# Spreading projection and gate units over two attention phases, and summing squares on another engine, in a hybrid decoder layer

## The reference

```python
z = rmsnorm(x, g_mix) @ w_in        # split: mq mk mv | mo | mi mf | fq fk fv | ff | ga gb
fq, fk = rmsnorm(fq, g_qn), rmsnorm(fk, g_kn)      # per head of 64
# mLSTM, per head and chunk of 128 positions
w_intra = exp(dlog - m_t[..., None]);  w_inter = exp(a - m_t)
s = einsum('bhtd,bhsd->bhts', q, k) * w_intra
num = w_inter * einsum('bhtd,bhde->bhte', q, c_st) + einsum('bhts,bhse->bhte', s, v)
den = w_inter * einsum('bhtd,bhd->bht', q, n_st) + sum(s, -1)
h = num / maximum(abs(den), exp(-m_t))
c_new = decay * c_st + einsum('bhs,bhsd,bhse->bhde', w_s, k, v)
# attention, per head and block of 128 queries
logits = einsum('bthd,bshd->bhts', qb, k) * F_SCALE + fb - f_keys      # causal
yf = einsum('bhts,bshd->bthd', softmax(logits), v)
# merge, FFN, embedding
hm = rmsnorm(y_m, g_mh) * sigmoid(mo)
x = x + (sigmoid(ga) * (hm @ w_pa) + sigmoid(gb) * (yf @ w_pb)) @ w_out
gu = rmsnorm(x, g_ffn) @ w_gu
x = x + (silu(gu[..., :D_FF]) * gu[..., D_FF:]) @ w_down
y = x + sigmoid(rmsnorm(x, g_ple) @ w_ple_gate) * (p @ w_ple_proj)
```

## Time and profile before

| | us |
| --- | --- |
| median of 3 runs (lowest, highest) | 2348.0 (2345.8, 2350.44) |
| the profiled execution, its own time | 2341.82 |
| its span in the trace | 2340.2 |
| TensorE busy in the span | 2082.0 (89%) |
| DVE, ACT, POOL busy | 886.7, 534.1, 575.8 |

### The profile page before, as it was taken

How to read it: one execution, slowest core, us unless ns; L and a number is a source line. 1 busy time by engine, 2 the same in 40 slices (tenths; PEclk the granted TensorE clock), 3 DMA queues, 4 the chain that set the end, 5 groups by cost and what they waited for, 6 DMA issues and landing times.

```text
span 2340.2 us, 33231 instructions
## 1 busy us (share of the span) xinstructions
PE 2082.0 (89%) x12507; PEld 1902.8 (81%) x12507; DVE 886.7 (38%) x1525; ACT 534.1 (23%) x845; POOL 575.8 (25%) x391
## 2 busy tenths in 40 slices
PE   2999997999968988947788999999999999998888
PEld 2877776999957777734687989999999999998688
DVE  4500001323346666642374323443344433444433
ACT  5212112221144454411532220011000110001311
POOL 0312222111122131100222242323223232320521
PEclk9999998998989898967899999999999999999999
DMA  3222215443222222146632121111111111100121
GB/s 120 68 80 108 88 43 165 131 138 114 76 55 77 63 72 63 49 157 217 206 117 64 36 72 37 44 46 42 47 36 54 36 54 36 45 27 27 48 71 37
DMA packets 203827, 179.44 MB, mean 77 GB/s; under 512 B 49114, under 2 KB 168126, under 8 KB 203746
## 3 DMA queue, kind: packets, MB, share of 16 engines
q1 hardware_dynamic: 154594, 151.28, 20.5%
q10 hardware_dynamic: 48160, 27.40, 3.9%
q0 software_dynamic: 1024, 0.13, 0.1%
HBM read 141.68 MB, written 39.26 MB: 77 GB/s over the span
## 4 chain that ended last, share of the span: by engine, by line
PE 76%; DVE 8%; issue 7%; ACT 2%; DMA 2%; POOL 2%; SPq 1%; ACTq 1%; DVEq 0%; POOLq 0%
PE pair L2164 23%; PE bank L2164 19%; PE bank L1860 9%; PE bank L1887 7%; PE pair L1860 4%; PE pair L2001 2%; PE pair L1975 1%; DVE dd L1475 1%; PE pair L1985 1%; PE pair L1974 1%; DVE ptl L1522 1%; PE pair L2054 1%; POOL tmp L949 1%; PE pair L1963 1%; DVE XR L1789 1%
## 5 line engine op out<-in xcount | busy, mean ns | idle before, releaser
L2164 PE MATMUL bank<-acth,wha 128*128 128x352 f32 x640 | 213.3, 333 | 30.0 <-DVE actl L1683 17.1
L2164 PE MATMUL bank<-actl,wha 128*128 128x352 f32 x640 | 210.5, 329 | 0.0
L2164 PE MATMUL bank<-acth,wla 128*128 128x352 f32 x640 | 210.5, 329 | 0.0
L2164 PE MATMUL pair<-hh,whb 128*128 128x352 f32 x528 | 173.5, 329 | 24.2 <-DVE XR L1789 23.7
L915 POOL CAST wha<-raw 128x1024 fp32r<-128x1024 f32 x46 | 52.1, 1132 | 523.2 <-PE pair L2164 190.5
L1887 PE MATMUL bank<-acth,fwh 128*128 128x352 f32 x480 | 172.2, 359 | 3.4 <-POOL fwl L835 3.4
L2164 PE MATMUL pair<-hl,whb 128*128 128x352 f32 x528 | 169.2, 320 | 0.0
L2164 PE MATMUL pair<-hh,wlb 128*128 128x352 f32 x528 | 169.2, 320 | 0.0
L1789 DVE TENSOR_TENSOR XR<-XR,pair 128x352 f32<-128x352 f32 x264 | 134.2, 518 | 81.4 <-PE pair L2164 81.2
L1887 PE MATMUL bank<-actl,fwh 128*128 128x352 f32 x480 | 165.0, 344 | 0.0
L1887 PE MATMUL bank<-acth,fwl 128*128 128x352 f32 x480 | 164.5, 343 | 0.0
(11 more groups left out here) (422 smaller groups left out, 5066.9 us busy)
## 6 DMA issues: line engine op xcount, KB each, us to landing
raw<-in_w_gu SPq DMA_DIRECT2D x44, 512.0 KB, 3.9
wraw<-in_w_in SPq DMA_DIRECT2D x24, 512.0 KB, 4.8
scratch_zA<-stage SPq DMA_DIRECT2D x48, 256.0 KB, 2.0
raw<-in_w_down SPq DMA_DIRECT2D x22, 512.0 KB, 3.3
scratch_zT<-fout ACTq DMA_DIRECT2D x20, 528.0 KB, 2.7
fraw<-in_w_in SPq DMA_DIRECT2D x20, 512.0 KB, 4.3
gs<-scratch_zT SPq DMA_DIRECT2D x16, 528.0 KB, 3.5
kpg<-in_cache_k SPq DMA_DIRECT2D x32, 256.0 KB, 4.8
```

The source lines that it names most:

```text
L2164: ins = nc.tensor.matmul(out, w[i](k), x[j](k), start=n == 0, stop=n == total - 1)
```

## The change

Phase 1 keeps 27 of the projection units, the three groups of the mLSTM. The 27 units of the attention's q, k, v (`f_unit`) run two ahead of the meeting before phase 2, one behind it, and the others in the mLSTM heads, where the nine gate units of each head stood. Their weights lie in a ring of five pieces; the first four are split in phase 1, the other eight by POOL alone (`split_unit_weights`, a copy and a subtraction a piece). In phase 2 SP loads q and k ahead of v, and the rows right behind.

All 60 gate units go to phase 3: four ahead of the first head and seven in each, as 14 halves. Their weights have two buffers instead of three; the stores of the gates go from ACT's queue to SP's, together with those of `yb`. The low part of the keys, `klo`, gets 128 rows.

In phase 5 POOL adds up the squares in `rv` (`sum_squares`), and three products with ones at the end replace L2207 and L2212. In phase 7 pin is loaded early; the low part on DVE and the squares on ACT run within the last FFN group; POOL splits the first embedding weights and then adds up the squares of two thirds of the columns, the last third goes through ones as before; the first two units of products run ahead of the sums. Loops of TensorE, ACT, POOL and SP in phases 1 to 3 and the last one of TensorE are written out.

The core of the diff, by phase and engine.

Phase 2, TensorE:

```diff
+            pe.wait_ge(unit_out, MG * XTILES)
+            f_unit(0)
+            f_unit(1)
             begin_phase(pe, 2)
+            f_unit(2)
...
+            for g in range(HM):
+                u0, wide = 7 * g, 7 * g + 6 < UNITS
+                if g:
+                    f_unit(u0)
+                pe.wait_ge(qk_in, 64 * g + 64)
...
-                gate_unit(g, 0, 3)
-                gate_unit(g, 1, 3)
+                if g:
+                    f_unit(u0 + 1)
+                    f_unit(u0 + 2)
...
-                for f in range(6, 9):
-                    gate_unit(g, f, 3)
```

Phase 2, POOL:

```diff
+            pool_mlstm(0)
+            split_unit_weights(4)
+            pool_mlstm(1)
+            for n in range(5, 9):
+                split_unit_weights(n)
+            pool_mlstm(2)
+            for n in range(9, 12):
+                split_unit_weights(n)
+            pool_mlstm(3)
```

Phase 3, SP:

```diff
+            for g in range(HF):
+                for u in range(PRE + 7 * g if g else 0, PRE + 7 * g + 7):
+                    if u % 3 == 2:
+                        store_gate(u // 3)
+                        if u // 3 + 3 < NGATE // 3:
+                            load_gate(u // 3 + 3)
+                    if u == PRE + 7 * g + 4 and g:
+                        store_y(g - 1)
+                if g < HF - 1:
+                    load_row(g + 1)
```

Phase 3, TensorE and DVE:

```diff
                 logits3(g, 2)
                 turn_p3(g, 0)
+                gate(h + 3)
                 logits3(g, 3)
                 turn_p3(g, 1)
+                gate(h + 4)
...
-                nc.vector.tensor_tensor(klo[:], pB[0:DH, :], khh[0:DH, :].bitcast(F32), ALU.subtract).then_inc(qk_lo, 1)
+                nc.vector.tensor_tensor(klo[:], pB[:], khh[:].bitcast(F32), ALU.subtract).then_inc(qk_lo, 1)
```

Phase 5, POOL and TensorE:

```diff
+            def sum_squares(first, wait):
+                for t in range(NT):
+                    pool.wait_ge(sq5, wait + t + 1)
+                    nc.gpsimd.tensor_tensor(rv[:, t, :], rv[:, t, :], sqt[:, t, :], ALU.add).then_inc(sq5_add, 1)
...
+                    split_piece(g * 2 + 10 + j, g + 6, j, wha[:, j], wla[:, j])
+                    sum_squares(j, g * 6 + 3 * j)
...
-                    if u == 3:
-                        sums(0)
-                sums(1)
```

Phase 7, POOL:

```diff
-                nc.gpsimd.tensor_tensor(sqt[:, n % 3, :], x, x, ALU.mult).then_inc(sq7, 1)
+            for j in range(2):
+                ple_weights(0, j)
+            for m in range(2 * (KC - 1)):
+                t, c = m // (KC - 1), m % (KC - 1) + 1
+                pool.wait_ge(sq7, t * KC + c + 1)
+                nc.gpsimd.tensor_tensor(rv[:, t, :], rv[:, t, :], sqt[:, m % 3, :], ALU.add).then_inc(sq7_add, 1)
```

More of the change, by code:

```diff
@@ L360, in program @@
         nst_t = sem("nst_t")
-        fw_in = [sem(f"fw_in{i}") for i in range(3)]
+        fw_in = [sem(f"fw_in{i}") for i in range(2)]
         f_hi = sem("f_hi")
@@ L1974, in logits3 @@
                     nc.tensor.matmul(out[:, c:c + w], q, khh[:, c:c + w], start=True, stop=False)
-                    ins = nc.tensor.matmul(out[:, c:c + w], q[0:DH, :], klo[:, c:c + w], start=False, stop=not last)
+                    ins = nc.tensor.matmul(out[:, c:c + w], q, klo[:, c:c + w], start=False, stop=not last)
                     if last:
@@ L2032, in pe_head @@
                 values3(g, 2)
+                gate(h + 11)
+                gate(h + 12)
                 turn_p3(g, 7)
-                gate(2, 1)
+                gate(h + 13)
                 values3(g, 3)
             pe.wait_ge(consts, 3)
-            with pe.Fori(0, HF - 1) as g:
+            for h in range(2 * PRE):
+                gate(h)
+            for g in range(HF):
                 pe_head(g)
-            pe_head(HF - 1)
             end_phase(pe)
@@ L2204, in _ @@
             pe.wait_ge(t_lo, 3 * KC)
-            pe.wait_ge(rv_zero, 1)
-            for t in range(NT):
-                nc.tensor.matmul(BANK[4 + t][:, 0:TW], ones[:], rv[:, t, :], start=True, stop=False)
             with pe.Fori(0, KC // 2) as g:
-                def sums(j):
-                    for t in range(NT):
-                        pe.wait_ge(sq5, g * 6 + 3 * j + t + 1)
-                        nc.tensor.matmul(BANK[4 + t][:, 0:TW], ones[:], sqt[:, t, :], start=False, stop=False).then_inc(ss5_mm, 1)
                 for u in range(6):
@@ L2255, in _ @@
                     nc.tensor.transpose(PAIR[2 * k][:, i * P:(i + 1) * P], pin[:, i, k * P:(k + 1) * P], ident[:])
-                nc.tensor.transpose(BANK[k][:, 0:NS], pin[0:NS, NCH, k * P:(k + 1) * P], ident[0:NS, 0:NS]).then_inc(pt7_mm, 1)
-            for n in range(NT * KC):
-                t, c = n // KC, n % KC
-                if n == 2 * KC:
-                    pe.wait_ge(pt7_lo, 2)
-                pe.wait_ge(sq7, n + 1)
-                nc.tensor.matmul(BANK[4 + t][:, 0:TW], ones[:], sqt[:, n % 3, :], start=c == 0, stop=c == KC - 1).then_inc(ss7_mm, 1)
@@ new lines, in square_sums @@
+            def square_sums(t):
+                if t < 2:
+                    pe.wait_ge(sq7_add, (t + 1) * (KC - 1))
+                    nc.tensor.matmul(BANK[4 + t][:, 0:TW], ones[:], rv[:, t, :], start=True, stop=True).then_inc(ss7_mm, 1)
+                    return
+                for c in range(KC):
+                    pe.wait_ge(sq7, 2 * KC + c + 1)
+                    nc.tensor.matmul(BANK[6][:, 0:TW], ones[:], sqt[:, (2 * (KC - 1) + c) % 3, :], start=c == 0, stop=c == KC - 1).then_inc(ss7_mm, 1)
```

691 lines of the change are left out of this document (390 added, 301 removed).

## The result

The changed kernel takes 2239.0 us at the median (2237.1 to 2244.7), the kernel before 2346.9 beside it: a ratio of 0.955, with a 95% interval of 0.952 to 0.958. The forecast was 2272, in a range of 2236 to 2312. The profiled execution took 2240.1 us (span 2238.5), 101.7 less than the one of before, where the sum had 76.2. The lines of the page and of the views that answer to those of before follow.

What follows compares the result with a forecast made beforehand. TensorE was taken to bound the kernel, with slack in mLSTM, attention and the embedding's start. Gains 9 + 40 + 12.7 + 14.5 = 76.2 us; 2341.8 - 76.2 = 2265.6, with 6.2 to the median 2272 us; range 2236 to 2312.

Steps and rivals of the forecast that it cites:

- Projections: Projection stage: 27 of 54 units, 5.57 us each, move 150.4 us to the mLSTM stage; by itself neither gain nor loss.
- mLSTM: mLSTM stage: gains of 27.6 us from waits and cold clock, losses of 18.6, net gain 9; bounds -5 to +24.
- head 0's bare chain: mLSTM head 0: no unit between transposes and score products, so TensorE waits 5.3 us, plus 2.5 for a cold re-entry.
- The step on head 1: mLSTM: unit 9's pieces come late behind POOL's mask additions, 7.4 us and 1 for the clock; head 2 loses 2.4.
- Attention: Attention stage: gate halves cover the waits and lift the clock to 1.00; gain 40 us, bounds 0 to 56.
- The additional rows cost nothing: Attention: klo on 128 rows streams as many columns and DVE subtracts as many, so no cost was counted.
- the heads' own work: Attention: 182.8 us at full clock, 22.9 a head, kept the same in the sum for after the change.
- The two stalls of 6 us in heads 3 and 6: Attention: the store of y waits behind a gate store, delaying yb and row maxima; 16 us with clock in both heads.
- Rival 2: The charged stalls (y store 16, POOL's pieces 11, head 0's 7.8 half) don't come: 2238 us; chance 0.15.
- rival 4: Clock in mLSTM and attention falls instead of rising; at 0.85 it costs 81 us more: 2353 us, slower; chance 0.07.
- Output projection: Squares' sums leave TensorE, POOL's additions hidden beside products except the last; net gain 12.7 us, bounds 5 to 16.
- rival 3: POOL's additions hold back weight splits or squares; output projection and embedding gain nothing: 2299 us; chance 0.07.

Runs made afterwards that it cites:

- pieces_first: The changed kernel with POOL splitting weight pieces 5 to 7 ahead of the mask additions of mLSTM head 1, not behind them: 2242.8 us.
- klo64: The changed kernel with the low part of the keys on 64 rows again, as before the change: 2268.9 us.
- y_swap: The changed kernel with the store of y moved ahead of the gate store that falls on the same unit: 2221.3 us.
- gates_bundled: The changed kernel with all 14 gate halves of each attention head in one row, ACT's evictions with them, not between score blocks: 2350.1 us.
- sums_on_pe: The changed kernel with the output projection's squares summed by ones on TensorE as before, none on POOL: 2254.1 us.
- embedding_before: The changed kernel with the embedding's start (pin's load, squares, low parts, sums, weight split) as in the kernel before: 2257.0 us.
- the best version: The changed kernel with y_swap, unit 9 behind head 1's scores and states, and POOL's first weight split held until head 0's scores are made: 2213.7 us.

## Why the prediction was right, and where it was off

- **Projections**: right; the unit's price held (148.7 us left for 27 units, 150.4 counted).
- **mLSTM**: 6.9 against 9. The waits that I took from the order came where I had put them: head 0's bare chain 7.0 (5.3 counted), the ring 10.7 (7.4 + 2.4 counted), the gap 9.3 (12.5 counted). Two things were missing: DVE's qs took 3.15 us beside POOL (below), and a wait of 2.0 for cnew at the end. The step on head 1 had the time right (7.7 in head 1 and 2.9 in head 2) and the cause half: POOL's order is one limit and the ring's size the other, and pieces_first showed that lifting the first alone gains nothing. No run takes this stage's part of the change back alone, so its 6.9 us rest on the trace. The rule of the Trainium skill on POOL's slower additions ("GPSIMD Engine Reference", § 3.1), weighed there, stays open: no run here had the splits on DVE.
- **Attention**: this is the step that failed, by size and not by sign. "The additional rows cost nothing" was true, but I counted what klo's additional rows might cost and not what they might save, and they are worth 27 to 30 us: klo64 puts the stage back to 38 us of gain, where I had 40, and the kernel to 2269, where I had 2272. The mistake was to take the heads' own work, 22.9 us a head, as the same in both kernels. The Trainium skill would have told: "TensorEngine Tiling (Array Packing)", the section on key properties, says that a change of the tiling mode drains the engine. If a product of 64 rows between ones of 128 is such a change, this case's traces agree, at 0.1 to 0.2 us for each; a drain itself isn't seen in them, only the later start.
- The two stalls of 6 us in heads 3 and 6 were 6.69 and 6.61, 16 us with the clock in the sum and 17.7 by y_swap. Rival 2, that the charged stalls don't come, gave 2238 and so nearly the measured time, but for the wrong reason: they all came. That 2239 lies in the range at all is luck: its lower end, 2236, was there for rival 2, and the gain from klo, which filled that place, was in no bound.
- **The clock**: 0.98 in attention; rival 4 was wrong there. The Trainium skill ("TensorE: Matmul & The Clock Gate", Part 4) says that transposes don't count as busy in the same way; that they would hold attention at 0.93, as I weighed it, doesn't show here: the heads have as many transposes as before, and with gate halves between them the clock is up. In the mLSTM it hardly rose, from 0.89 to 0.90. gates_bundled shows attention's clock at 0.88 when the waits come back.
- **Output projection**: 13.5 in the trace and 15 by sums_on_pe, against 12.7. The cover that I named, products beside POOL's additions, held; rival 3 falls by this run and the next.
- **Embedding**: 16 in the trace and 18 by embedding_before, against 14.5. DVE's residual ended 2.8 us later behind the FFN's last product (4 counted), the third unit began 27 us behind it (26 counted).
- **Slips in the sums**: POOL's additions in head 1 are 4.6 us by the rows, not 4.7; the output projection's terms give 12.6, the embedding's 14.3; the third unit before began at 2205.3, not 2204. These move the forecast by 1 us or so. Rival 2 with head 0's 7.8 halved is 31 and not 34, so 2241.

## What to carry to other kernels

Dense work put between the steps of a latency chain is worth its place, not its presence: with the same 56 units the kernel took 2239 us when they stood as halves between the blocks and 2350 when they stood in one row a head. Look at the distance from one matmul's start to the next, not at durations, wherever, as here, tiles of different row counts alternate, and try padding the smaller one if its missing half can be had. In a queue that carries two kinds of stores, a store on which a buffer's reuse hangs goes ahead of the one that nobody waits for, but not so far ahead that the queue stands waiting for it.

## What the runs showed of the hardware that I had not expected

A change between matmuls of 64 and of 128 rows cost 0.1 to 0.2 us each time (30 us of klo64 over its 192 changes is 0.16): there the next weights are loaded only as their own matmul starts, not while the last one streams (rows of klo above). And DVE slows down beside POOL: qs (128 x 1056) took 3.15 us in the changed kernel, while POOL split a piece from 247.09 to 249.44, 1.65 in the kernel before with a part of POOL's addition beside it, and 1.26 in the best version with POOL idle. The rows of the changed kernel, DVE and POOL, then POOL's of the kernel before, then DVE's of the best version:

```profile
247.41 3.15 DVE L1541 TENSOR_TENSOR qs<-qT,aB 128x1056 f32<-128x1056 f32 x1 [3.47 <-ACT kT L1151]
...
247.09 2.35 POOL L909 TENSOR_TENSOR ring<-wraw,ring 128x1024 fp32r<-128x1024 f32 x1
```

```profile
398.52 1.89 POOL L845 TENSOR_TENSOR rB<-rB,gcur 128x1024 f32<-128x1024 f32 x1
```

```profile
245.51 1.26 DVE L1542 TENSOR_TENSOR qs<-qT,aB 128x1056 f32<-128x1056 f32 x1 [3.15 <-ACT kT L1152]
```

In both pairs qs ends 1.12 us behind the end of POOL's instruction (250.56 behind 249.44, 401.53 behind 400.41), nearly the time that it takes alone: by these rows it makes next to no headway while POOL's instruction runs. The Trainium skill ("GPSIMD Engine Reference", § 1) has the two share their way to the memory, with contention when a DVE instruction has two inputs there, as qs does; these rows agree, but no run sets the shared way apart from another cause.
